# Twelve slots for expert weights in place of eleven, and a new order of work around the first expert picks of a two-block model

## The reference

```python
q = (x @ wq).reshape(B, L, 8, 2, 128)
s = einsum('blhpd,hpkd->blhpk', q, keys)          # two scores of 128 keys per head
ts, ti = top_k(s, 16)
cand = ts[..., 0, :, None] + ts[..., 1, None, :]   # 16 x 16 sums
cs, ci = top_k(cand.reshape(..., 256), 16)
experts = ti[0][ci // 16] * 128 + ti[1][ci % 16]
act = gelu(x . u_tab[experts]) * softmax(cs)
out = sum over picks of act * v_tab[experts]
```

## Time and profile before

| | us |
|---|---|
| median of 3 runs | 2091.91 (2090.76 to 2094.72) |
| span of the profiled execution, first to last instruction | 2089.1 |
| PE busy | 1768.7 (85%) |
| VectorE busy | 771.6 (37%) |
| ScalarE busy | 423.4 (20%) |
| GpSimd busy | 299.1 (14%) |
| moved by DMA | 761.80 MB, mean 365 GB/s |

### The profile page before, as it was taken

One profiled execution on the slowest core, in us unless ns is written; L12 is line 12 of the kernel. 1 busy time (PEld: TensorE's weight loads), 2 busy tenths in 40 slices (PEclk: granted clock), 3 DMA queues, 4 the chain that ended last, 5 costly groups with the idle time before them and its releaser, 6 DMA issues. The chain is left out here.

```text
span 2089.1 us, 23422 instructions
## 1 busy us (share of the span) xinstructions
PE 1768.7 (85%) x9328; PEld 914.3 (44%) x9328; DVE 771.6 (37%) x1877; ACT 423.4 (20%) x990; POOL 299.1 (14%) x284
## 2 busy tenths in 40 slices
PE   9999986886766555668999999888799999998886
PEld 7779862553321111124554444233377544442332
DVE  3955176776667777854230000000213300000002
ACT  2481122221222112223121010000123201110001
POOL 0000033453334444440000000000000000000000
PEclk9999998998886876689999999999999999999999
DMA  7236279999999999997789999999944999999996
GB/s 262 93 131 290 101 299 388 409 415 422 422 421 421 421 421 421 421 420 302 292 360 428 426 428 427 426 426 426 423 181 187 412 427 426 427 427 427 427 426 277
DMA packets 78973, 761.80 MB, mean 365 GB/s; under 512 B 8628, under 2 KB 9621, under 8 KB 17542
## 3 DMA queue, kind: packets, MB, share of 16 engines
q1 hardware_dynamic: 41190, 489.34, 56.1%
q0 software_dynamic: 37664, 270.84, 31.5%
HBM read 759.10 MB, written 1.05 MB: 364 GB/s over the span
## 5 line engine op out<-in xcount | busy, mean ns | idle before, releaser
L2584 PE MATMUL bank<-arena 128*64 128x512 f32 x3072 | 684.3, 599 | 55.3 <-DMA arena<-in_w_up 19.6
L1057 PE MATMUL bank<-arena 64*64 64x512 f32 x2032 | 324.6, 794 | 233.7 <-ACT arena L772 233.6
L2584 PEld LDWEIGHTS bank<-arena 128*64 128x64 f32 x3072 | 233.8, 138 | 492.0 <-issue 470.8
L563 POOL DMA_INDIRECT arena<-in_peer_uv,arena x256 | 287.4, 1123 | 631.5 <-PE bank L1057 305.9
L1401 DVE CUSTOM_DVE_ANT_0 arena<-arena 128x1024 f32<-128x1024 f32 x256 | 313.6, 1225 | 171.2 <-DMA arena<-in_peer_uv,arena 168.0
L1057 PEld LDWEIGHTS bank<-arena 64*64 64x64 f32 x2032 | 93.9, 177 | 444.8 <-ACT arena L772 265.7
L2711 DVE TENSOR_TENSOR arena<-arena,bank 128x512 f32<-128x512 f32 x32 | 22.0, 687 | 718.5 <-PE bank L2584 718.5
L822 PE MATMUL bank<-arena 128*128 128x272 f32 (+2 forms) x768 | 145.2, 349 | 0.5 <-ACT arena L596 0.3
L822 PEld LDWEIGHTS bank<-arena 128*128 128x128 f32 x768 | 126.4, 191 | 19.9 <-issue 2.5
L767 ACT ACTIVATE arena<-arena 128x4 f32<-128x4 f32 (+1 forms) x65 | 13.3, 205 | 466.4 <-DVE arena L1401 466.4
L1487 POOL DMA_DIRECT2D arena<-in_w_router x2 | 1.1, 574 | 562.4 <-POOLq L2469 528.0
(11 more groups left out here) (444 smaller groups left out, 1482.9 us busy)
## 6 DMA issues: line engine op xcount, KB each, us to landing
arena<-in_w_up SPq DMA_DIRECT2D x64, 2048.0 KB, 36.9
arena<-in_w_gate SPq DMA_DIRECT2D x64, 2048.0 KB, 32.9
arena<-in_w_down SPq DMA_DIRECT2D x64, 2048.0 KB, 39.0
arena<-in_w_in SPq DMA_DIRECT2D x13, 2048.0 KB, 8.5
arena<-in_w_out SPq DMA_DIRECT2D x2, 4096.0 KB, 17.9
arena<-in_wq SPq DMA_DIRECT2D x4, 2048.0 KB, 13.6
arena<-in_rg_out SPq DMA_DIRECT2D x1, 4096.0 KB, 13.9
arena<-in_peer_uv,arena POOLq DMA_INDIRECT x256, 17.4
```

The costliest lines, as they stand in the source:

```text
L563: nc.gpsimd.indirect_dma_start(SLOT[slot_of[j]], None, d["peer_uv"], bass.IndirectOffsetOnAxis(IDX[:, u % 4, k:k + 1], 0)).then_inc(s_row[ ...
L1057: m = pe.matmul(bank[banks[t][half]][to:to + HALF, :], DIAG[lo:lo + HALF, k + j, :], row[lo:lo + HALF, D + half * 512:D + (half + 1) * 512 ...
L2584: x = pe.matmul(bank[b][j * C:(j + 1) * C, :], operand[:, c, j * C:(j + 1) * C], RING[s % AHEAD][:, c % (DC // 2), j, :], start=(c == 0), ...
```

## The change

- `MOE_SLOTS` 11 to 12 and `EARLY_SLOTS` 10 to 11. The arena grows from 50,900 to 54,616 columns (14,864 bytes a partition). The room comes from `dynamic_dma_scratch_size=2048`, which the kernel before left at its default, and from smaller router tables. Fixed columns of the gating stage move by the same amount.
- Which slots the gating and the dilated stage load when: the layer 0 load of slot 10 goes out right behind that of slot 4. In the dilated stage the weights lie in slots 1 to 6, the other buffers in 7 to 10, and slot 0 is loaded at the start of the stage.
- The norm parameters at the end of a MoE stage go to slot 0, which is free after step 85.
- The third load of query weights has room of its own (7 of 8 chunks in `ahead`), so it goes out behind the second. `rg_out`'s weights are loaded in two halves, each in its own region, so slots 4 and 5 come free after half of `rg_out(1)`.
- PE: two projection tiles instead of four ahead of `turn(0)`; the first queries of head 0 are split, each with one side (`QUERIES`); the other tiles come after the first scores.
- VectorE: the indices of unit 0 are found in two eights (`first_picks`), and GpSimd starts on picks 0 to 7 with the first. `route(1, ...)` moves behind group 0 and group 1. `merge(1, n)` moves by one place.

```diff
+DESCRIPTOR_RING = 2048
+COLS_ALL = 54616
...
-    WQ = [cut(base, P, DC, 4 * P) for base in (spec, spec + DC * 4 * P, scan, scan + DC * 4 * P)]
+    WQ_PARTS = [[(cut(base, P, DC, 4 * P), 0, DC)] for base in (spec, spec + DC * 4 * P, scan, scan + DC * 4 * P)]
+    WQ_PARTS[2] = [(cut(ahead, P, DC - 1, 4 * P), 0, DC - 1), (cut(scan + DC * D, P, 1, 4 * P), DC - 1, DC)]
...
-    QUERIES = ((0, 0, 0, 2, 4, 5), (0, 0, 2, 4, 6, 7)) + tuple(
+    QUERIES = ((0, 0, 0, 1, 4, 5), (0, 0, 1, 2, 6, 7), (0, 0, 2, 4, 4, 5)) + tuple(
...
-    QUERIES_AFTER = {0: 3, **{g + 1: g for g in range(4, NQ)}}
+    QUERIES_AFTER = {0: 3, 1: 4, **{g: g for g in range(5, NQ)}}
...
+    FIRST_ORDER = (2, 3, 0, 1, 4, 5, 6, 7)
+    FREE_AFTER_TILES = {2: PROJ_TILES + 4, 0: PROJ_TILES + LATE_TILES}
+    FREE_AFTER_BRANCH = {4: 3, 6: 4}
...
             query_weights(1)
+            query_weights(2)
             sp.wait_ge(s_wm, 4)
-            query_weights(2)
             query_weights(3)
...
-            pool.wait_ge(s_mm, PROJ_TILES + LATE_TILES)
             for u in range(UNITS):
-                pool.wait_ge(s_idx, u + 1)
+                pool.wait_ge(s_idx, u + 2 if u else 1)
                 for k in range(R):
                     j = u * R + k
+                    if j == R // 2:
+                        pool.wait_ge(s_idx, 2)
                     if freed[j] is not None:
                         pool.wait_ge(s_pv, freed[j] + 1)
-                    elif slot_of[j] == 4:
-                        pool.wait_ge(s_rom, 4)
+                    elif slot_of[j] in FREE_AFTER_TILES:
+                        pool.wait_ge(s_mm, FREE_AFTER_TILES[slot_of[j]])
+                    elif slot_of[j] in FREE_AFTER_BRANCH:
+                        pool.wait_ge(s_rom, FREE_AFTER_BRANCH[slot_of[j]])
...
-            for n in range(PROJ_TILES, PROJ_TILES + 4):
+            for n in range(PROJ_TILES, PROJ_TILES + 2):
                 tile(n)
             te.wait_ge(s_res, 2)
             turn(0)
-            tile(PROJ_TILES + 4)
+            tile(PROJ_TILES + 2)
             queries(0)
-            tile(PROJ_TILES + 5)
+            queries(1)
             te.wait_ge(s_keys, 16)
             scores(0)
-            queries(1)
-            tile(PROJ_TILES + 6)
+            tile(PROJ_TILES + 3)
             scores(1)
-            tile(PROJ_TILES + 7)
+            for n in range(PROJ_TILES + 4, PROJ_TILES + LATE_TILES):
+                tile(n)
             rg_out(1)
             queries(2)
...
+            def first_picks(n):
+
+                half = R // 2
+                ks = slice(n * half, (n + 1) * half)
+                wide = [P, 2, half, R]
+                if n:
+                    step(v.match_replace(CAND, CS[:, 0:half], CAND, -BIG))
+                step(v.max(CS[:, ks], CAND))
+                m = v.max_index(CI[:, ks], CS[:, ks], CAND)
...
+                step(v.tensor_scalar(CJ[:, 0, ks], CI[:, ks], 4, None, ALU.logical_shift_right))
+                step(v.tensor_scalar(CJ[:, 1, ks], CI[:, ks], 15, None, ALU.bitwise_and))
+                step(v.tensor_copy(CF[:, :, ks], CJ[:, :, ks]))
+                step(v.tensor_tensor(EQ_FIRST, CF[:, :, ks].unsqueeze(3).to_broadcast(wide),
+                                     IOTA.unsqueeze(1).unsqueeze(1).to_broadcast(wide), ALU.is_equal))
+                step(v.tensor_tensor(EQ_FIRST, EQ_FIRST, TIF.unsqueeze(2).to_broadcast(wide), ALU.mult))
+                step(v.tensor_reduce(E12[:, :, ks], EQ_FIRST, X_AXIS, ALU.add))
+                v.scalar_tensor_tensor(IDX[:, 0, ks], E12[:, 0, ks], float(NKEYS), E12[:, 1, ks], ALU.mult, ALU.add).then_inc(s_idx, 1)
...
                     if j == 2:
-                        merge(1, 1)
-                    if j == Q:
-                        route(1, 2)
+                        ve.wait_ge(s_ev, PROJ_TILES + LATE_TILES)
+                        merge(1, 0)
...
-            for part in range(4):
+            for part in range(2):
                 route(0, part)
-            ve.wait_ge(s_ev, PROJ_TILES + LATE_TILES)
-            route(1, 0)
-            route(1, 1)
-            merge(1, 0)
+            for n in range(2):
+                first_picks(n)
...
-                    if n == 1:
-                        route(1, 3)
+                    if n == 0:
+                        merge(1, 1)
+                    if n in (0, 1):
+                        route(1, 2 * n)
+                        route(1, 2 * n + 1)
...
-            experts(4)
+            experts(4, 10)
...
+            experts(0)
             sp.wait_ge(s_pm, VALUE_JOBS)
-            experts(9)
+            experts(2)
             sp.wait_ge(s_pm, job("k", DPAIRS - 1) + 1)
-            experts(0, 1)
+            experts(3, 4)
             sp.wait_ge(s_pm, len(JOBS))
-            experts(2, 3, 8)
+            experts(1, 5, 6)
             sp.wait_ge(s_sm, HEADS)
             sp.wait_ge(s_sc, HEADS)
-            experts(4, 5)
+            experts(7, 8)
             sp.wait_ge(s_om, 4)
-            experts(6)
+            experts(9)
             sp.wait_ge(router.s_mm, LOGITS_MM + TT)
-            experts(7)
+            experts(10)
...
-MOE_SLOTS = 11
-EARLY_SLOTS = 10
+MOE_SLOTS = 12
+EARLY_SLOTS = 11
+PARAM_SLOT = 0
```

More of the change, by code:

```diff
@@ L262, in front_stage @@
     spec = at.take(DC * D)
+    ahead = at.take((DC - 1) * 4 * P + 8 * R + 4)
     nT = at.take(DC * L)
@@ L295, in front_stage @@
     assert tmps + 2 * D_HY <= spec
-    RGOUT = cut(early, P, DC, D)
+    RGOUT = [cut(early + n * DC * 4 * P, P, DC, 4 * P) for n in range(2)]
     KSP = cut(spec, P, 2, 3, D_HY)
@@ L349, in front_stage @@
     DOTS, GELU, WGT = (cut(late.take(UNITS * R), P, UNITS, R) for n in range(3))
-    IDX = cut(scan + DC * D, P, 4, R).bitcast(U32)
-    EXPS = cut(scan + DC * D + 4 * R, P, 4, R)
+    held = ahead + (DC - 1) * 4 * P
+    IDX = cut(held, P, 4, R).bitcast(U32)
+    EXPS = cut(held + 4 * R, P, 4, R)
     MEMT = cut(scan + KV_COLS, P, DC, T)
@@ L414, in front_stage, with scored @@
         last[s] = j
-    def scored(u):
+    def scored(u, side):
         t, h = u // PH, u % PH
         for g, (qt, k, lo, hi, _, _) in enumerate(QUERIES):
-            if (qt, k) == (t, h // 2) and lo <= h % 2 * 2 < hi:
+            if (qt, k) == (t, h // 2) and lo <= h % 2 * 2 + side < hi:
                 return g + 1
@@ L1480, in __init__ @@
         self.SUMW, self.GWB = (cut(at.take(2 * NE), P, 2 * NE) for _ in range(2))
-        self.LGT = cut(at.take(TT * NE), P, TT, NE)
+        self.LGT, self.SEL, self.OH = (cut(at.take(TT * NE), P, TT, NE) for _ in range(3))
+        self.PAIR = cut(at.take(8 * 6), P, 8, 6)
+        self.GS8, self.M8, self.E8F, self.G8 = (cut(at.take(16), P, TT, 8) for _ in range(4))
+        self.E8, self.GI8 = (cut(at.take(16), P, TT, 8).bitcast(U32) for _ in range(2))
+        self.GRPF = cut(at.take(2), P, 2)
         self.s_in, self.s_cst = sem("router_in"), sem("router_constants")
@@ L1595, in vector_choose @@
             do(v.max_index(GI8[:, t, :], G8[:, t, :], GS8[:, t, :]))
-        do(v.tensor_copy(K.GRPF, GI8[:, :, 0]))
-        do(v.tensor_tensor(OH, both(self.GRP), wide(K.GRPF), ALU.not_equal))
+        do(v.tensor_copy(self.GRPF, GI8[:, :, 0]))
+        do(v.tensor_tensor(OH, both(self.GRP), wide(self.GRPF), ALU.not_equal))
         do(v.scalar_tensor_tensor(SEL, OH, -BIG, SEL, ALU.mult, ALU.add))
@@ L1912, in _ @@
             ve.wait_ge(s_par, 32)
-            do(v.memset(K.GS8, -BIG))
+            do(v.memset(router.GS8, -BIG))
             for t in range(TT):
@@ L2490, in _ @@
                 names = ("w_v", "w_k", "w_in1")
-                for n, (to, name, later) in enumerate(zip(dilated_weights(K), names, (0, 3, 5))):
+                for n, (to, name, later) in enumerate(zip(dilated_weights(K), names, (0, 2, 4))):
                     sp.wait_ge(s_step, steps + later if later else steps)
@@ L2783, in build @@
         route = Room(ROUTE_COLS)
-        K.IOTA = cut(route.take(P), P, P)
+        K.IOTA = cut(route.take(PACK_ROWS), P, PACK_ROWS)
         K.RK, K.GT = (cut(route.take(TT * PASSES * NE), P, TT, PASSES * NE) for _ in range(2))
-        K.PRB, K.MSK, K.SEL, K.OH, K.TMPA, K.TMPB = (cut(route.take(TT * NE), P, TT, NE) for _ in range(6))
-        K.PAIR = cut(route.take(8 * 6), P, 8, 6)
-        K.GS8, K.M8, K.E8F, K.G8 = (cut(route.take(16), P, TT, 8) for _ in range(4))
-        K.E8, K.GI8 = (cut(route.take(16), P, TT, 8).bitcast(U32) for _ in range(2))
-        K.NM_, K.SUMS, K.RS, K.GRPF = (cut(route.take(2), P, 2) for _ in range(4))
+        K.PRB, K.MSK, K.TMPA, K.TMPB = (cut(route.take(TT * NE), P, TT, NE) for _ in range(4))
+        K.NM_, K.SUMS, K.RS = (cut(route.take(2), P, 2) for _ in range(3))
         K.CNT, K.NPF = (cut(route.take(1), P, 1) for _ in range(2))
```

100 lines of the change are left out of this document (57 added, 43 removed).

## The result

In the runs taken with the prediction the changed kernel took 2076.21 us (median of 4, 2073.87 to 2078.75) beside 2093.31 us before (2090.76 to 2097.42): a ratio of 0.9917, 95% interval 0.9898 to 0.9937, or 17.4 us faster by that ratio (the two medians differ by 17.1). The forecast was 2080.1 us against 2091.9, a ratio of 0.9944, just outside the interval. The time lies inside the forecast's range. The slots do what was forecast; of the steps that lead to the gain of the picks the last one failed, and the gain is larger than its 11.8 us. Over all its 15 runs the median is 2076.8 us, over all 49 of the kernel before 2091.7, so 15 us is the better figure for the gain.

The account below looks back on a forecast made before the run. The bound was taken to be DMA transfers at their rate plus stretches with idle DMA engines. Slots 9.84 us plus picks 2.0 us made 11.8 us, a profiled span of 2077.3 and a forecast of 2080.1 us, range 2071 to 2088.

Parts of the forecast that it names:

- The slots, 9.84 us: Gating and dilated stages: in each layer one 2 MiB expert load of 4.92 us moves into idle DMA time.
- Params, dilated weights, tables: nothing: Norm parameters, `w_k` and `w_in1` still go out behind the expert loads, and tables get smaller: no time gained or lost.
- The first pick, 7.6 us: Start of the picks: fewer tiles ahead and a shorter first search send pick 0 at 264.6 instead of 272.19 us.
- Steps 1 to 3: Picks 0 to 15: `rg_out` halves release picks 4 to 7; group 0's sums start at 286.9, group 1's at 297.6 us.
- Step 4: PE behind group 1: output weights plus 3.74 us of added queries put group 2's sums at 314.4, pick 16 1.4 us later.
- Step 5: DMA queue near 324 us: one query load fewer, 4.9 us shorter; picks 3.5 us ahead by pick 24.
- Step 6: VectorE: `residual(1)` and `route(3, 0)` hold up group 5's dots; 1.9 of 3.5 us lead left at pick 28, then kept.
- a lead outside 0 to 4 us: Sign at pick 32: the forecast is wrong if the lead over the kernel before isn't 0 to 4 us.
- The head start arrives: Rival: PE's queue behind group 1 has room for the added queries; picks gain 5 to 12.5 us, 2070 to 2077; chance 0.16.
- The picks lose: Rival: slots bring 9.8 us but the picks cost 0 to 5, giving 2082 to 2087 us; chance 0.10.
- a slot brings nothing: Rival: in one or both layers the added load meets other transfers; gain 2 to 7 us or none, 2085 to 2093; chance 0.12.
- The descriptor memory: Rival: GpSimd's 2048 bytes fill and must run empty 21 times at 3.3 us, 70 in all, giving 2150 us; chance 0.10.

Follow-up runs that it names:

- e12: The changed kernel with layer 1's two output-weight products on PE put behind score groups 3 and 4 instead of 1 and 2: 2082.22 us, ratio 0.9955.
- e1: The kernel before with only the twelve slots and what they need, picks starting in the old order: 2080.04 us, ratio 0.9942.

## Why the prediction was right, and what was off

- **The bound** held. Plateaus of 420 and 426 GB/s stand in both kernels, and each gain or loss shown above is a load moved into or out of a valley, or a valley among the first picks that grew or shrank. One reading of the earlier trace rows was off by a slice: slice 7 has 409 GB/s, and the plateau of 415 and more begins with the next.
- **The slots, 9.84 us.** The profiles give 4.9 us in layer 0 and about 5 in layer 1 once the late landing is left out, as forecast. The times say 12.1, between 9.0 and 15.1, which holds the term without proving it to a microsecond. PE did not take over: 22.8 and 22.3 us of idle time remain. The prediction writes of three loads ahead of the wait for the key projections; they are two, slot 0 and slot 2, and its sum counts them so.
- **Params, dilated weights, tables: nothing.** Consistent with 0.1 us between the two MoE stages; not tested alone.
- **The first pick, 7.6 us.** It was 8.7: it went at 263.49 (forecast 264.6). The first score came at 255.49 (forecast 255.9).
- **Steps 1 to 3** held within 1.6 us in the first profile: picks 4 and 6 at 271.65 and 278.80 (272.4, 279.6), group 0's sums 285.56 (286.9) with PE waiting for the `merge` as forecast, group 1's 296.02 (297.6). In the changed kernel's two other profiles group 1's sums begin at 294.99 and 295.20, 2.6 and 2.4 us ahead of the forecast.
- **Step 4** named the right instructions and was 2.0 us too pessimistic: group 2's sums at 312.39 for 314.4. Most of this came in with the earlier groups. In the two other profiles it is 4.7 and 4.5 (309.66 and 309.88), and pick 16 goes at 312.4 and 312.6 against the sign "not before 315". Putting the output weights behind groups 2 and 3 shows the mechanism by taking it away.
- **Step 5** is the whole gain of the front, and its 4.9 us were nearly the right size: the load early is worth 4.0 us at pick 32 without any head start, and some 3.5 us in the time (2079.9 over the 12 runs of slots only and load late, 2076.8 and 2075.9 for the changed kernel and the slots with the load early). I had 3.5 us by pick 24; the first profile has 0.8 (341.59 for 342.38), with pick 19's dot, at 335.16 for 335.96, still 4.30 us behind the one load that is left. The two others have 3.0 and 4.0, so the place of this gain is told by none of them alone.
- **Step 6** failed, and with it the size of the term. I let `residual(1)` and `route(3, 0)` hold up group 5's dots and take 1.6 of 3.5 us by pick 28. The first profile is 3.2 us ahead at pick 28 (354.26 for 357.48) and 3.7 at pick 32 (363.51 for 367.25): behind pick 24 the lead grows where I had it shrink, and it grows by 2.4 to 2.7 us up to pick 28 in all three profiles. `residual(1)` and `route(3, 0)` do hold up the group's first dot (343.71 for 344.80), but the kernel before had that delay too and then waited for the group's last rows until 351.05. With the load early these had landed, so the last dot gained 3.5 us; I had counted the delay on VectorE and left out the wait behind it that goes away. In the two other profiles the lead at pick 32 is 5.7 and 8.1 us. The prediction had named a lead outside 0 to 4 us as a sign of being wrong, and for the picks it is one.
- **Sum**: 9.84 + 2.0 was forecast; 11.8 + 3.5, about 15 us, is what the pooled times give. The first 17.4 had chance in it. That the picks' 2.0 came near at all is partly luck: a loss of 1.4 us by pick 16 was taken off that wasn't there, and so were the 1.6 us of step 6, while the load brought less than its 4.9.
- **Rivals.** "The head start arrives" fell as a mechanism (the load early without a head start does as well), though the time came out inside its reach. "The picks lose" fell by the new front alone (0.9987), "a slot brings nothing" by the slots alone (0.9942). The descriptor memory fell by the kernel before with 2048 bytes, 0.9998.

The last dot of the picks lies at 957.4 us (mean of 4 profiles) with the load late and 951.4 (7 profiles) with it early, 6.0 us, while the times show some 3.5. Part of this is which executions were profiled: the four were on average 2.3 us above the median of their own kernel, the seven 0.1 us below. If such deviations lie ahead of the last dot, 3.5 are left, as in the times. It stays open whether they do, since one kernel alone spreads over nearly 5 us there (948.37 to 953.22).

## What to carry to other kernels

Where the transfers are the bound, count what a change moves into moments when the DMA engines are idle; an earlier start of the first consumer, here 8.7 us, can be worth nothing unless each later link of the chain, other engines' fixed queue order included, moves too. One load of 2 MiB taken out of a full queue and put where the queue was empty did what three reordered engines did not. And a piece of filler work may be moved later only up to the first instruction, on any engine, that waits for its result.

## What the runs showed of the hardware

- The gathers cost GpSimd nothing more with 2048 bytes of descriptor memory (0.9998; 1108 ns an issue beside 1123). At 1024 bytes issues come one transfer, 2.5 us, apart, and the 121 us of longer issues and waits only took the place of other waits.
- One group's 32 matmuls on PE took 3.66 us at a granted clock of 1.00 and 5.36 us where its mean was 0.66 to 0.72. Behind 2.28 idle us both were seen, so which group pays changes from one execution to the next of the same kernel. The longest were 5.87 us behind 10.69 idle us (experiment e12) and 6.61 behind 4.93 (e1, granted clock 0.55 in 301 to 308).
- Gathers by index reached 420 to 421 GB/s over hundreds of microseconds, 1.4% below the 427 GB/s of the large direct loads.
